# The output gate's product moved from the projection stage into the recurrence's loop, its sigmoid into the mix stage

## The reference, cut to what matters

```
z = h @ w_in + b_in
q, k, v, o, gt, ga, gb = jnp.split(z, IN_SPLITS, axis=-1)     # o: (tokens, 512)
u = ga * jax.nn.sigmoid(gb)                                   # input of the convolution
...
num = (jnp.einsum('bhcts,bhcsv->bhctv', s, vc)                # s: scores times decay, in a chunk
       + e_int[..., None] * jnp.einsum('bhcvk,bhctk->bhctv', C_prev, qc))
h = num / jnp.maximum(jnp.abs(den), jnp.exp(-m_t))[..., None]
...
hn = h * lax.rsqrt(jnp.mean(h * h, axis=-1, keepdims=True) + EPS) * norm_g
return hn.transpose(0, 2, 1, 3).reshape(B, T, H * dv) * jax.nn.sigmoid(o)
```

## Time and profile before

| what | us |
|---|---|
| median of 3 runs | 3175.64 (3172.88 to 3181.79) |
| profiled execution, span from first to last instruction | 3178.9 |
| end of the projection: "o" products to last k_tok copy | 347.7 to 407.2 |
| recurrence stage until the first output step's first product | 407.5 to 434.6 |
| output steps, first to last product on TensorE | 434.6 to 548.5 |
| mix stage | 554.8 to 569.4 |

### The profile page before, as it was taken

How to read it: one execution, slowest core, us unless ns; L and a number is a source line. 1 busy time by engine, 2 the same in 40 slices (tenths; PEclk the granted TensorE clock), 3 DMA queues, 4 the chain that set the end, 5 groups by cost and what they waited for, 6 DMA issues and landing times. The chain is left out here.

```text
span 3178.9 us, 38607 instructions
## 1 busy us (share of the span) xinstructions
PE 2742.0 (86%) x11910; PEld 1925.6 (61%) x11911; DVE 1643.3 (52%) x2421; ACT 1222.6 (38%) x1726; POOL 922.0 (29%) x1092
## 2 busy tenths in 40 slices
PE   5999988787599999999989947999968999865997
PEld 2455456673277777777767733456655666754776
DVE  3767756653365466666675632245462111545653
ACT  2320135420066466666665631026222111315653
POOL 0850032225343333334333320166120000104333
PEclk8999965887799999999999978999989999977999
DMA  6430000322367789888797744000202110426972
GB/s 249 150 126 1 27 1 1 149 93 104 137 227 259 223 271 323 256 288 310 264 318 241 212 141 146 27 1 1 43 14 60 40 40 20 163 88 234 306 225 51
DMA packets 159037, 463.18 MB, mean 146 GB/s; under 512 B 37948, under 2 KB 67248, under 8 KB 138184
## 3 DMA queue, kind: packets, MB, share of 16 engines
q1 hardware_dynamic: 115280, 357.72, 30.3%
q0 software_dynamic: 43264, 104.02, 13.9%
q10 hardware_dynamic: 392, 0.14, 0.0%
HBM read 414.05 MB, written 91.62 MB: 159 GB/s over the span
## 5 line engine op out<-in xcount | busy, mean ns | idle before, releaser
L1937 DVE TENSOR_TENSOR moe_low<-moe_raw,moe_high 128x2048 fp32r<-128x2048 f32 x160 | 359.9, 2289 | 80.4 <-ACT moe_high L1882 57.4
L1847 PE MATMUL psum<-moe_high,moe_xg_high 128*128 128x512 f32 x960 | 389.9, 406 | 6.2 <-issue 3.2
L1849 PE MATMUL psum<-moe_high,moe_xg_low 128*128 128x512 f32 x960 | 378.2, 394 | 0.0
L1848 PE MATMUL psum<-moe_low,moe_xg_high 128*128 128x512 f32 x960 | 375.5, 391 | 0.0
L1783 POOL DMA_INDIRECT moe_acc<-moe_y_blk,moe_is_now x97 | 208.3, 2147 | 307.9 <-DMA moe_acc<-moe_y_blk,moe_is_now 274.8
L1882 ACT ACTIVATE moe_high<-moe_raw 128x2048 fp32r<-128x2048 f32 x160 | 297.6, 1915 | 0.1
L1894 ACT ACTIVATE moe_y_blk<-psum,row_w 128x1024 f32 x124 | 138.1, 1113 | 239.3 <-DMA moe_acc<-moe_y_blk,moe_is_now 135.1
L1834 PE MATMUL psum<-moe_high_down,moe_hid_high 128*128 x488 | 207.0, 424 | 14.6 <-DVE moe_hid_low L1946 14.0
L1821 PE MATMUL psum<-ident,moe_xg 128*128 128x128 f32 x976 | 133.4, 281 | 95.8 <-DMA moe_xg<-moe_rows,moe_ig_now 95.0
L1847 PEld LDWEIGHTS psum<-moe_high,moe_xg_high 128*128 128x128 f32 x960 | 181.6, 189 | 43.4 <-issue 4.7
L1849 PEld LDWEIGHTS psum<-moe_high,moe_xg_low 128*128 128x128 f32 x960 | 180.8, 188 | 43.1
(11 more groups left out here) (585 smaller groups left out, 5030.0 us busy)
## 6 DMA issues: line engine op xcount, KB each, us to landing
moe_raw<-in_we_gate SPq DMA_DIRECT2D x64, 1024.0 KB
moe_raw<-in_we_up SPq DMA_DIRECT2D x64, 1024.0 KB
moe_raw<-in_we_down SPq DMA_DIRECT2D x64, 1024.0 KB, 7.8
x<-in_w_ada POOLq DMA_DIRECT2D x16, 1024.0 KB, 5.6
moe_raw<-in_w_e_gate SPq DMA_DIRECT2D x16, 1024.0 KB
moe_raw<-in_w_e_up SPq DMA_DIRECT2D x16, 1024.0 KB
moe_raw<-in_w_e_down SPq DMA_DIRECT2D x16, 1024.0 KB
w_ring<-in_w_in SPq DMA_DIRECT2D x12, 1024.0 KB, 7.6
```

The lines of the kernel that those rows point to most:

```text
L1847: pe.matmul(to, x_hi, R(of_k(w_hi, k)), start=(k == 0), stop=False)
L1848: pe.matmul(to, x_hi, R(of_k(w_lo, k)), start=False, stop=False)
L1849: last = pe.matmul(to, x_lo, R(of_k(w_hi, k)), start=False, stop=(k == KD - 1))
L1937: dve.tensor_tensor(R(low[:, at:at + 2048]), raw[r][:, part], hi, ALU.subtract).then_inc(w_low, 1)
```

## The change

The entries "o" leave the plan, with their bias addition on VectorE and their sigmoid on ScalarE. Their weights are still loaded in the projection, into the same slot; the bias comes as one row `s.b_o` of 512 values on one partition. In the recurrence a new function `gate_product(i)` lays one of 64 products: tile i // 8, contraction part i % 8; before each tile's first it adds the bias as a product of ones with the row b_o. Step v lays number 2v behind the numerator and number 2v + 1 at its end. They accumulate in bank 7, so the state's update moves to bank 1 (`local`), and the scores of both heads go to bank 0, one after the other, with the numerator's two products between and behind them. ScalarE copies each finished tile out (`move_gate`, at the start of step 4, 8, ..., and once after the loop). The squares of y go to the buffer x instead of hT, which the gate's products still read. The sigmoid of all 8 tiles is applied at the start of the mix stage.

```diff
-    plan += [("o", t, 0) for t in range(NT)] + [("kt", t, 0) for t in range(STEPS)]
+    plan += [("kt", t, 0) for t in range(STEPS)]
...
-                sp.dma_start(b_o, A["b_in"][0:1, C_O:C_O + 512].to_broadcast([P, 512])).then_inc(biases_in, 16)
+                sp.dma_start(s.b_o[:, :], A["b_in"][0:1, C_O:C_O + 512]).then_inc(biases_in, 16)
...
-                    elif kind == "o":
-                        if i == first["o"]:
-                            dve.wait_ge(later.added, 2 * later.KH * later.TILES)
-                        c.then(dve.tensor_tensor(s.sig_o[:, a, :], bank[:, :], b_o, ALU.add))
-                        c.wait(dve)
-                        moved = dve.sem_inc(moved_v, 1)
-                        dve.sem_inc(o_added, 1)
-                        continue
...
-                    if kind == "o":
-                        act.wait_ge(o_added, a + 1)
-                        s.act_c.then(act.activation(s.sig_o[:, a, :], s.sig_o[:, a, :], ACT.Sigmoid))
...
-    sqy = s.hT[:, 0:KC, :]
+    sqy = s.x[:, NT // 2:NT, :]
+    w_o = s.mixer_weights.ring[:, 1]
+    local = s.bank[1][:, 0:W]
...
-                def scores(v):
+                def scores(v, i):
                     j, d, k = pairs[P0 + v]
                     t0 = tile_of(j, d) * P
-                    for i in range(2):
-                        last = pe.matmul(s.bank[i][:, 0:P], s.qkT[lanes(i), 2 + k, t0:t0 + P], s.qkT[lanes(i), k, t0:t0 + P],
-                                         start=True, stop=True)
-                    last.then_inc(scores_done, 1)
+                    if i == 1:
+                        pe.wait_ge(scores_done, 2 * v + 1)
+                    pe.matmul(s.bank[0][:, i * P:(i + 1) * P], s.qkT[lanes(i), 2 + k, t0:t0 + P], s.qkT[lanes(i), k, t0:t0 + P],
+                              start=True, stop=True).then_inc(scores_done, 1)
+
+                def gate_product(i):
+                    t, k = divmod(i, KD)
+                    if k == 0:
+                        if t == 0:
+                            pe.wait_ge(s.mixer_weights.ready["o"], 32)
+                        else:
+                            pe.wait_ge(o_moved, t)
+                        pe.matmul(s.bank[7][:, :], s.ones[0:1, :], s.b_o[:, :], start=True, stop=False)
+                    last = pe.matmul(s.bank[7][:, :], s.hT[:, k, t * P:(t + 1) * P], w_o[:, k], start=False, stop=(k == KD - 1))
+                    if k == KD - 1:
+                        last.then_inc(o_done, 1)
...
                         pe.wait_ge(pt_ready, v + 1)
-                        if v + 1 < NV:
-                            scores(v + 1)
                         for i in range(2):
+                            if v + 1 < NV:
+                                scores(v + 1, i)
                             last = pe.matmul(s.bank[bank + i][:, 0:W], pt[:, v % 2, i, :], s.v_aug[:, tile_of(j, d), 2 * k + i, :],
                                              start=True, stop=True)
                         last.then_inc(num_done, 1)
+                        gate_product(2 * v)
...
+                    if v >= 0:
+                        gate_product(2 * v + 1)
...
+                def move_gate(t):
+                    act.wait_ge(o_done, t + 1)
+                    act.activation(s.sig_o[:, t, :], s.bank[7], ACT.Copy).then_inc(o_moved, 1)
...
                 for v in range(NV):
                     j, d, k = pairs[P0 + v]
+                    if v % 4 == 0 and v:
+                        move_gate(v // 4 - 1)
...
+                move_gate(NT - 1)
                 act.wait_ge(out_done, 1)
...
             for t in range(NT):
+                dve.wait_ge(sig_ready, t + 1)
                 for h in range(H1):
...
             act.activation(s.hs[:, :], s.hs[:, :], ACT.Sqrt).then_inc(h_root, 1)
+            for t in range(NT):
+                act.activation(s.sig_o[:, t, :], s.sig_o[:, t, :], ACT.Sigmoid).then_inc(sig_ready, 1)
```

More of the change, by code:

```diff
@@ L458, in stage_project @@
         place.append(count[kind in by_act])
-    first = {kind: min(i for i, p in enumerate(plan) if p[0] == kind) for kind in ("qk", "v", "kt", "gt", "o", "ga", "gb")}
-    last_of = {kind: max(i for i, p in enumerate(plan) if p[0] == kind) for kind in ("qk", "v", "kt", "gt", "o", "ga", "gb")}
+    first = {kind: min(i for i, p in enumerate(plan) if p[0] == kind) for kind in ("qk", "v", "kt", "gt", "ga", "gb")}
+    last_of = {kind: max(i for i, p in enumerate(plan) if p[0] == kind) for kind in ("qk", "v", "kt", "gt", "ga", "gb")}
     gated = [i for i, entry in enumerate(plan) if entry[0] == "ga"]
@@ L466, in stage_project @@
         tile_done, moved_v, moved_a = sem(s, "proj_tile_done"), sem(s, "proj_moved_v"), sem(s, "proj_moved_a")
-        o_added, sig_ready, pads_set = sem(s, "o_added"), sem(s, "sig_ready"), sem(s, "pads_set")
+        sig_ready, pads_set = sem(s, "sig_ready"), sem(s, "pads_set")
         gates = Gates(s)
-        b_v, b_o = s.x[:, 0, 0:512], s.x[:, 0, 512:1024]
+        b_v = s.x[:, 0, 0:512]
         sig = s.x[:, 1, :].rearrange("p (b n) -> p b n", b=2)
@@ L503, in _ @@
                         pe.wait_ge(moved_a if plan[i - 8][0] in by_act else moved_v, place[i - 8])
-                    if kind in ("qk", "v", "gt", "o") and i == first[kind]:
+                    if kind in ("qk", "v", "gt") and i == first[kind]:
                         pe.wait_ge(w_ready[kind], 16 if kind == "gt" else 32)
@@ L511, in _ @@
                         last = gates.tensor(pe, a, bank)
-                    elif kind in ("v", "gt", "o"):
+                    elif kind in ("v", "gt"):
                         h = s.hcT[:, :, (a - NT) * P:(a - NT + 1) * P] if a >= NT else s.hT[:, :, a * P:(a + 1) * P]
@@ L800, in mixer_inputs @@
     s.hs = sb("hs", [P, NT * H1])
+    s.b_o = sb("b_o", [1, 512])
     stage_project(s)
@@ L837, in stage_mlstm @@
         y_inv, y_root, y_done, out_done = (sem(s, f"y_{x}") for x in ("inv", "root", "done", "out_done"))
+        o_done, o_moved = sem(s, "m_o_done"), sem(s, "m_o_moved")
         sq = sb("m_sq", [P, P])
@@ L893, in _ @@
                         pe.wait_ge(maxima_set, 1)
+                        scores(0, 0)
                         maxima(0)
-                        scores(0)
+                        scores(0, 1)
                     if v >= 0:
@@ L919, in _ @@
                             h = 2 * k + i
-                            last = pe.matmul(s.bank[7][lanes(i), 0:W], s.k_tok[:, tile_of(j, d), h * DK:(h + 1) * DK],
+                            last = pe.matmul(local[lanes(i), :], s.k_tok[:, tile_of(j, d), h * DK:(h + 1) * DK],
                                              wv[:, p % 2, i, :], start=True, stop=True)
                         last.then_inc(local_done, 1)
+                    if v >= 0:
+                        gate_product(2 * v + 1)
             @block.scalar
@@ L1001, in weights @@
                     dve.wait_ge(exp_ready, 2 * (v + 1))
-                    dve.wait_ge(scores_done, v + 1)
+                    dve.wait_ge(scores_done, 2 * (v + 1))
                     if v >= 2:
                         dve.wait_ge(num_done, v - 1)
-                    dve.tensor_tensor(pt[:, v % 2, :, :], both(0)[:, :, 0:P], decay[:, v // 2 % 2, 2 * k:2 * k + 2, :],
+                    dve.tensor_tensor(pt[:, v % 2, :, :], s.bank[0][:, 0:2 * P].rearrange("p (i n) -> p i n", i=2), decay[:, v // 2 % 2, 2 * k:2 * k + 2, :],
                                       ALU.mult).then_inc(pt_ready, 1)
@@ L1034, in _ @@
                         C = state[:, d, k, :]
-                        dve.scalar_tensor_tensor(C, C, EA2[:, j, d, k:k + 1], s.bank[7][:, 0:W],
+                        dve.scalar_tensor_tensor(C, C, EA2[:, j, d, k:k + 1], local,
                                                  ALU.mult, ALU.add).then_inc(state_moved, 1)
```

1 line of the change is left out of this document (added).

## The result

| | median us | runs | lowest to highest |
|---|---|---|---|
| before | 3177.72 | 4 | 3172.88 to 3181.79 |
| changed | 3206.72 | 4 | 3201.38 to 3208.92 |

The ratio is 1.0083, its 95% interval 1.0067 to 1.0100: the change makes the kernel slower, by more than the 0.3% that can be told. It lies above the forecast (3174.6) and above the range (3161 to 3200).

What follows compares the result with a forecast made beforehand. TensorE was taken to bound the projection's end before, VectorE's taps after, and TensorE nearly all the recurrence after. Terms -18.1 + 0.5 + 11.3 + 2 + 0 + 3.3 = -1.0 us gave 3174.6, range 3161 to 3200.

Steps and rivals of the forecast that it cites:

- What bounds the kernel: TensorE bounds the projection's end; in the recurrence VectorE and ScalarE's loop first, TensorE near the end, at granted 0.50.
- The projection, -18: Projection's end: 54.9 us of TensorE removed, but VectorE's taps then end the stage, so 18.1 come off; bounds -17 and -19.
- The start, +0.5: Start of the recurrence stage: sums over y start cold after TensorE idles, 9.3 us instead of 8.80; ends -1.9 and +4.9.
- The recurrence, +11.3: Output steps: gate and bias products make TensorE the bound, two steps take 8.04 us, 125.2 against 113.9; bounds +5 and +21.
- second rival: Recurrence: each step's second score waits for the first on TensorE; at 0.6 a step +15, 3190; chance 0.12.
- The clock, +2: Recurrence: wide gate products raise and hold TensorE's clock level, with one cold spell costing about 2.4; bounds 0 and +6.
- Waits of the gate, 0: Recurrence: ScalarE's copies of bank 7 stay hidden beside TensorE's work, costing 0; if not hidden, 0.3 x 7.
- The mix, +3.3: Mix stage: 8 sigmoids and a table load on ScalarE, 6.1 us less 2.8 of waits; bounds +2 and +6.
- Rivals 1 and 3: Recurrence: 1, products fill TensorE's waits, 3164, chance 0.20; 3, the clock stays low, 3289 or 3231, chance 0.13.

Runs made afterwards that it cites:

- second experiment: Changed kernel, but in steps 29 and 30 alone scores go back to two banks, ahead of the numerator, without wait; 3213.02 us in one run, those steps 3.01.
- third experiment: Changed kernel, but step 29 alternates scores and numerator in two banks without wait, step 30 uses one bank with wait, no alternation; 3172.85 us, steps 3.61 and 3.54.
- five tile kernel: Changed kernel, but five gate tiles stay in the projection, three go into steps 0 to 11, GpSimd adds the bias, then two-bank scores; 3152.42 us, ratio 0.9993.
- first experiment: Changed kernel without the one-row bias product before each gate tile's first product; 3194.27 us, ratio 1.0042, recurrence 139.91.
- last kernel: Five gate tiles and their bias products in the projection, one score product for both heads; against its predecessor, one gate product a step in steps 0 to 23; ratio 0.9950.

## Why the prediction was wrong

- *What bounds the kernel.* Right: the projection's end by TensorE before and by the taps after; in the loop TensorE becomes the bound.
- *The projection, -18.* Right: -19.2, just outside the -17 to -19 that I gave. The scatter of the stage's start between kernels is larger than the miss.
- *The start, +0.5.* +1.0: 9.68 for the sixteen instructions against my 9.3.
- *The recurrence, +11.3.* **This step failed, at the sentence "I take 0.1 a step; bounds 0, and 0.4, about a whole L872 drained and begun again."** The form of the scores costs 0.60 a step, above my upper bound. I counted the semaphore's wait and not the overlap that goes with it; and I held the overlap worthless at the full level because the four L872 are issued in 0.42 there. Those four follow a product of 80 rows (L864 in the earlier trace rows); behind the state's part, as in the loop, they take 0.32, and the numerator 0.55 (second experiment). The sum, 0.87, is as I had it, and the new form takes 1.48, where I had 0.97. Once the two heads' products are apart, the weight loads at three changes of shape begin only with their own products (the rows of the weight loads); how much of the 0.60 they are was not measured. It was the mechanism of my second rival, priced there at 0.6 a step and 3190, with a chance of 0.12; I gave it too little because I argued that the numerator in between covers the wait. The third experiment shows that it is no cover but a cost of its own (step 29, no wait: 3.61).
- The miss of 29.1 by terms, worked out from the profiles: the form, 31 x (0.60 - 0.10) = 15.5; the bias products, 8 x (1.25 - 0.86) = 3.1; the clock, below, 7.4; and 0.22 for two steps, 14 times, = 3.1, which no experiment names. It is mostly the gate's products among narrow ones: in a step without the maxima the one behind the numerator takes 0.95 (438.48 to 439.43), and the one at the step's end 1.06 (435.62 to 436.68), instead of twice 0.429 each; L909's 0.32, less than my 0.42, gives a part back.
- *The clock, +2.* The mechanism held in this loop: with the wide products it ran at the upper level for the most part, and without them at 0.50. That nothing else can raise the level is not shown (0.99 above in the five tile kernel, without them). The size was off: one cold spell was in the sum, and there are four. The first step is 11.51 - 5.89 - 0.83 (the wait for pt) = 4.8 too long, the steps 20, 24 and 28 by 7.45 - 5.89 = 1.56, 1.56 and, with its missing state update allowed for, 6.98 - 5.89 + 0.37 = 1.46: 9.4 instead of 2. 6.4 of them went with the bias product (first experiment), which I had as plain TensorE time.
- *Waits of the gate, 0.* Right, no row of TensorE shows one.
- *The mix, +3.3.* +2.5. The load before the sigmoids is there (580.55), and the first sigmoid starts 0.01 us after its end. What the prediction weighed under the Trainium skill, "ScalarE: Activation LUTs", "What ACT_TABLE_LOAD costs", a drain of 1.38 at each switch, is again not to be seen; with it the total would have been -1.0 + 1.4 = +0.4, not the +1 that I wrote.
- Rivals 1 and 3 are out: no pace of 7.5, and the level came up.
- The sum of rival 2 still fell short: 3190 against 3206.72. Its 15 us are the form; most of the rest is the bias products (3.1), the cold spells (7.4) and the 3.1 that no experiment names.

## What to carry to other kernels

Two half-height products of two heads, issued back to back into two banks, run over each other; a shared bank with a wait, or a full-height product put between them, ends that and costs about 0.6 us a step here, more than the 0.32 that the overlapped pair takes. Where only one bank is to be had, a zero-padded operand that makes them one full-height product is cheaper (0.98 against 1.48 with the numerator, 0.40 in the whole step). Work moved off a stage that another engine would end anyway gains only up to that engine: here 5 of 8 tiles could stay for 2 to 4 us. Of the ways to lay the three that moved, one product a step had the lowest ratio, but the runs don't tell it from two a step.

## What the runs showed of the hardware that I had not expected

- TensorE's granted level was 1.00 in a loop with waits (18.00 us with 14.23 busy, steps with one wide product each) and 0.50 in one without (82.00 of 82.00 busy, narrow products alone). The Trainium skill, "TensorE: Matmul & The Clock Gate", "Why this matters for your kernels", asks for TensorE to be kept busy; these two rows together don't agree with busy time as the measure. Nor do the gate's wide products alone decide: behind the last of them the five tile kernel still had 0.99 in 528 to 544, with TensorE busy 11.13 of 16. The first of the rows, from the last kernel:

```profile
432.00:450.00 18.00, 14.23 (x76) 8.48 (x76) 14.45 (x45) 5.31 (x17) 6.84 (x11) 1.00 0.00 1
```

- A product with one row of contraction and 512 columns added 1.25 to its step, where one with 128 rows takes 0.86 in a row of its like; placed behind the state's update it added 1.06 (5.70 - 4.64). The level fell behind it in steps 20, 24 and 28 of the changed kernel, in steps 4 and 8 of the one with the gate's products together, but not in the kernel with the scores in one product, nor in the projection that held five of them (1.00 in 346 to 386). So it is not the bias product alone; what decides is open.
- A tap of VectorE with two inputs in SBUF was held by about 0.89 us by one GpSimd addition of 512 columns: thirty taps took 44.04 with five additions beside them and 39.59 without.
